# A conditioned transformer on one core: the layers' modulation vectors computed beside the merge and the first feed-forward

## The reference

```python
cond = jax.nn.silu(c)
for l in range(2):
    mod = (cond @ ada_w[l] + ada_b[l])[:, None, :]          # ada_w[l]: 1024 x 6144
    shift_m, scale_m, gate_m, shift_f, scale_f, gate_f = jnp.split(mod, 6, axis=-1)
    h = rms_norm(x, norm_mix_g[l]) * (1.0 + scale_m) + shift_m
    ...                                                     # projection of h, two attentions, gated sum: y
    x = x + gate_m * y
    h = rms_norm(x, norm_mlp_g[l]) * (1.0 + scale_f) + shift_f
    x = x + gate_f * (jnp.square(jax.nn.relu(h @ w_mlp_up[l])) @ w_mlp_down[l])
```

## Time and profile before

| | us |
|---|---|
| median of 3 runs | 3493.77 (3490.32 to 3534.7) |
| the profiled execution's own time | 3522.62 |
| its span in the profile | 3520.8 |
| TensorE busy, matmuls | 3085.6 (88% of the span) |
| VectorE busy | 1684.8 (48%) |
| ScalarE busy | 1032.7 (29%) |
| mean granted TensorE clock | 0.875 of full speed |
| read from memory | 243.70 MB, 70 GB/s over the span |

### The profile page before, as it was taken

The page is one execution under the profiler, slowest core; times in us unless marked ns, Lnnn a source line. Parts: engine busy times, 40 slices in busy tenths (PEclk is TensorE's granted clock), DMA queues, the critical chain, the costliest instruction groups (busy, mean ns, idle before and its releaser), DMA issues. The chain is left out here.

```text
span 3520.8 us, 36278 instructions
## 1 busy us (share of the span) xinstructions
PE 3085.6 (88%) x14073; PEld 2379.1 (68%) x14073; DVE 1684.8 (48%) x3186; ACT 1032.7 (29%) x2010; POOL 19.2 (1%) x58
## 2 busy tenths in 40 slices
PE   7969378886999579989999899997998999989999
PEld 5866267774887147657777688863765777768887
DVE  3223555555443656674233444455757623344444
ACT  2223211112332134543332322212445323232221
POOL 0000100000000000000000000000000000000000
PEclk9975577777999789989599999998999968989999
DMA  3210000001333532102023222245220211322221
GB/s 121 85 16 1 11 8 1 1 1 45 95 100 109 187 142 72 49 13 69 20 59 111 72 96 96 96 153 206 72 72 1 64 37 39 106 72 96 96 96 48
DMA packets 210677, 249.45 MB, mean 71 GB/s; under 512 B 11759, under 2 KB 124362, under 8 KB 210506
## 3 DMA queue, kind: packets, MB, share of 16 engines
q1 hardware_dynamic: 202016, 243.63, 21.0%
q10 hardware_dynamic: 8490, 3.50, 0.5%
HBM read 243.70 MB, written 2.10 MB: 70 GB/s over the span
## 5 line engine op out<-in xcount | busy, mean ns | idle before, releaser
L1804 DVE TENSOR_TENSOR weights_lo<-weight_ring,weights_hi 128x512 fp32r<-128x512 f32 (+1 forms) x240 | 156.8, 656 | 350.0 <-ACT weights_hi L1789 350.0
L1789 ACT ACTIVATE weights_hi<-weight_ring 128x512 fp32r<-128x512 f32 (+1 forms) x240 | 143.9, 602 | 423.3 <-PE bank L1824 398.1
L1824 PE MATMUL bank<-h_hi,weights_hi 128*128 128x512 f32 x512 | 208.4, 407 | 16.0 <-DVE h_lo L1804 9.1
L722 PE MATMUL bank<-arena 64*128 64x512 f32 (+4 forms) x544 | 207.1, 620 | 17.4 <-PEq L905 11.0
L2661 PE MATMUL bank<-h_hi,weights_hi 128*128 128x512 f32 x512 | 202.4, 395 | 19.4 <-DVE h_lo L342 19.4
L2161 PE MATMUL bank<-chunk_hi,h_hi 128*128 128x512 f32 x448 | 185.2, 413 | 30.4 <-DVE h_lo L342 26.0
L2592 ACT ACTIVATE weights_hi<-weight_ring 128x1024 fp32r<-128x1024 f32 x128 | 135.3, 1057 | 259.4 <-PE bank L2661 258.8
L1824 PE MATMUL bank<-h_lo,weights_hi 128*128 128x512 f32 x512 | 204.0, 398 | 0.0
L2661 PE MATMUL bank<-h_lo,weights_hi 128*128 128x512 f32 x512 | 203.9, 398 | 0.0
L1824 PE MATMUL bank<-h_hi,weights_lo 128*128 128x512 f32 x512 | 201.5, 394 | 0.0
L2661 PE MATMUL bank<-h_hi,weights_lo 128*128 128x512 f32 x512 | 201.2, 393 | 0.0
(11 more groups left out here) (447 smaller groups left out, 5932.2 us busy)
## 6 DMA issues: line engine op xcount, KB each, us to landing
weight_ring<-in_ada_w SPq DMA_DIRECT2D x24, 2048.0 KB, 8.9
weight_ring<-in_w_in SPq DMA_DIRECT2D x21, 2048.0 KB, 7.8
weight_ring<-in_w_in SPq DMA_DIRECT2D x65, 512.0 KB, 5.1
weight_ring<-in_w_mlp_up SPq DMA_DIRECT2D x16, 2048.0 KB, 8.4
weight_ring<-in_w_mlp_down SPq DMA_DIRECT2D x16, 2048.0 KB, 7.8
weight_ring<-in_w_out SPq DMA_DIRECT2D x6, 2048.0 KB, 7.9
weight_ring<-in_w_in SPq DMA_DIRECT2D x10, 1024.0 KB, 6.8
weight_ring<-in_w_branch_a SPq DMA_DIRECT2D x16, 512.0 KB, 6.3
```

Of the source, the lines that this page charges most:

```text
L722: ins = pe.matmul(self.bank[q % S_BANKS][:, lo:lo + m], lhsT, rhs, start=True, stop=True)
L1789: act.activation(hi, src, ACT.Copy).then_inc(*hi_done.one())
L1804: dve.tensor_tensor(lo, src, hi.bitcast(F32), ALU.subtract).then_inc(*lo_done.one())
L1824: ins = pe.matmul(out, ws[a_][:, n % PIECES, k - k0, :], tile["x"][b_][:, k, :], start=k + a_ + b_ == 0, stop=last[n] and k == k1 - 1 and ...
```

## The change

The two modulation stages go. A new class `Modulation` is a "guest" of another stage: that of layer 0 in the merge, that of layer 1 in the feed-forward of layer 0. Its weights come in 24 half chunks of 1 MB (4 slices x 512 columns) into two buffers of its own, by DMAs that ScalarE issues. VectorE does all eight slices of a chunk (96 multiplies a layer, one in each piece of the merge, two in each tile of the feed-forward up to the 48th). TensorE does twelve "turns" a layer: four matmuls with 128 x 128 columns of `acc` as the stationary operand and a column of ones as the one moving column, which sum over the partitions and turn the result in one go, into bank 7. The hosts rotate seven banks in place of eight. Bias and gains are computed at the end of the host stage. `cond` is computed in the stage `sg`, and the copy of `hT` to `xT` moves to the end of ScalarE's list in `layer_tables`.

```diff
     for l in range(2):
-        for c in range(12):
-            plan.append((("ada", l, c), [(columns(a["ada_w_2"][l], c * 512, 512), 0)]))
...
+class Modulation:
+    HALVES = 24
+    OPS = 4
+    def load(self, eng):
+        k, q = self.kernel, self.loads
+        c, half = q // 2, q % 2
+        if q >= 2:
+            eng.wait_ge(*k.ada_used.at(q - 1))
+        eng.dma_start(self.w[:, half], columns(self.source, 512 * c, 512, 4 * half, 4)).then_inc(*k.ada_landed[half].dma())
+        self.loads += 1
+    def multiply(self, dve):
+        k, n = self.kernel, self.ops
+        q, j = n // 4, n % 4
+        c, half = q // 2, q % 2
+        acc, by = self.acc[:, c % 2, :], k.cond[:, 4 * half + j:4 * half + j + 1]
+        if j == 0:
+            dve.wait_ge(*k.ada_landed[half].at(16 * (c + 1)))
+        if n % 8 == 0:
+            if c >= 2:
+                dve.wait_ge(*k.mod_turned.at(c - 1))
+            ins = dve.tensor_scalar(acc, self.w[:, half, j, :], by, None, ALU.mult)
+        else:
+            dve.wait_ge(*self.previous)
+            ins = dve.scalar_tensor_tensor(acc, self.w[:, half, j, :], by, acc, ALU.mult, ALU.add)
...
+    def turn(self, pe):
+        k, c = self.kernel, self.turns
+        pe.wait_ge(*k.ada_used.at(2 * c + 2))
+        for j in range(4):
+            ins = pe.matmul(k.bank[7][:, 4 * c + j:4 * c + j + 1], self.acc[:, c % 2, j * P:(j + 1) * P], k.ones[:, 0:1],
+                            start=True, stop=True)
+        ins.then_inc(*k.mod_turned.one())
+        self.turns += 1
+    def finish(self, dve):
+        dve.wait_ge(*k.mod_turned.at(self.HALVES // 2))
+        dve.tensor_tensor(mod, k.bank[7][:, 0:48], k.par[:, b:b + 48], ALU.add).then_inc(*k.mod_row.one())
...
@@ spatial gating, ScalarE, before the Ln @@
+                act.activation(self.cond, self.par[:, PAR["c_2"]:PAR["c_2"] + ND], ACT.Silu).then_inc(*self.act_order.one())
@@ split_products @@
+        NB = 7 if guest else 8
@@ ScalarE @@
+                for _ in range(2 if guest else 0):
+                    guest.load(act)
                 for n in range(len(pieces) + PIECES):
+                    if guest and n >= 6 and (n - 6) % 4 == 0 and guest.loads < guest.HALVES:
+                        guest.load(act)
@@ VectorE, between the wait for piece n - 4 and the split of piece n @@
+                        if guest and guest.ops < guest.HALVES * guest.OPS:
+                            guest.multiply(dve)
@@ TensorE, ahead of piece n @@
+                    if guest and n >= 10 and (n - 10) % 8 == 0:
+                        guest.turn(pe)
...
+                while guest and guest.turns < guest.HALVES // 2:
+                    guest.turn(pe)
@@ layer_tables, ScalarE @@
-                act.activation(self.cond, self.par[:, PAR["c_2"]:PAR["c_2"] + ND], ACT.Silu)\
-                   .then_inc(*self.act_ready.step("cond"))
+                for k in range(ND):
+                    act.activation(self.xT[:, k, :], self.hT[:, k, :], ACT.Copy).then_inc(*self.evac_act.one())
@@ layer @@
-        self.modulation(l)
@@ mlp, ScalarE, after the split of tile t + 1 @@
+                    if guest and t >= 3 and t % 2 and guest.loads < guest.HALVES:
+                        guest.load(act)
@@ mlp, VectorE, after the split of tile t + 1 @@
+                    for _ in range(2 if guest and guest.ops < guest.HALVES * guest.OPS else 0):
+                        guest.multiply(dve)
@@ mlp, TensorE, ahead of tile t @@
+                    if guest and t >= 6 and (t - 6) % 4 == 0 and guest.turns < guest.HALVES // 2:
+                        guest.turn(pe)
```

More of the change, by code:

```diff
@@ L342, in second_part, with __init__ @@
         return dve.scalar_tensor_tensor(lo, self.dst[:, k, :], self.shift(k), hi.bitcast(F32), ALU.add, ALU.subtract)
+class Modulation:
+    HALVES = 24
+    OPS = 4
+    def __init__(self, kernel, l):
+        self.kernel, self.l = kernel, l
+        self.w, self.acc = kernel.take(2, 4, 512), kernel.take(2, 512)
+        self.source = kernel.a["ada_w_2"][l]
+        self.loads = self.ops = self.turns = 0
+    def load(self, eng):
[19 more added lines that the diff above has]
+            ins = dve.scalar_tensor_tensor(acc, self.w[:, half, j, :], by, acc, ALU.mult, ALU.add)
+        done = k.ada_used if j == 3 else k.mod_row
+        ins.then_inc(*done.one())
+        self.previous = done.all()
+        self.ops += 1
+    def turn(self, pe):
[7 more added lines that the diff above has]
+    def finish(self, dve):
+        k, l = self.kernel, self.l
+        assert self.ops == 4 * self.HALVES
+        dve.wait_ge(*k.mod_turned.at(self.HALVES // 2))
+        b = PAR["ada_b_2"] + 48 * l
+        mod = k.mods[:, l, :]
+        dve.tensor_tensor(mod, k.bank[7][:, 0:48], k.par[:, b:b + 48], ALU.add).then_inc(*k.mod_row.one())
+        dve.wait_ge(*k.mod_row.all())
+        for j, (at, name) in enumerate(((8, "norm_mix_g_2"), (32, "norm_mlp_g_2"))):
+            g = k.par[:, PAR[name] + 8 * l:PAR[name] + 8 * l + 8]
+            dve.scalar_tensor_tensor(k.gains[:, l, j, :], mod[:, at:at + 8], 1.0, g, ALU.add, ALU.mult)\
+                .then_inc(*k.mod_row.one())
@@ L395, in __init__ @@
         self.scratch = sb("scratch", [P, 512])
+        self.cond, self.mods, self.gains = sb("cond", [P, ND])[:], sb("modulations", [P, 2, 48]), sb("mod_gains", [P, 2, 2, ND])
+        self.ada_landed = [Signal(nc, f"ada_landed_{j}") for j in range(2)]
+        self.ada_used = Signal(nc, "ada_used")
+        self.mod_row = Signal(nc, "mod_row_ready")
+        self.mod_turned = Signal(nc, "mod_turned")
         self.nc_pos = sb("positions", [P, NT], I32)
@@ L1717, in recurrences, with split_products @@
         self.end_stage("rwkv")
-    def split_products(self, name, tiles, inputs, norm=None):
+    def split_products(self, name, tiles, inputs, norm=None, guest=None):
         nc = self.nc
-        NB = 8
+        NB = 7 if guest else 8
         PK, PIECES = 4, 4
@@ L1868, in gated_sum @@
                 readers.append(b)
-        self.split_products(name, tiles, inputs, norm)
+        self.split_products(name, tiles, inputs, norm, guest)
         self.top -= 2 * T
@@ L1888, in merge @@
             inputs[2 * i + 1] = self.by_k(ysT, y)[2 * i:2 * i + 2]
-        self.gated_sum("merge", mixT, plan, inputs, self.norm)
+        keep = self.top
+        guest = Modulation(self, 0)
+        self.gated_sum("merge", mixT, plan, inputs, self.norm, guest)
+        self.top = keep
         self.add_products("out", lambda c: ("out", c), mixT, None)
@@ L2561, in layer @@
         self.top = keep
[L2562 removed]
+        self.rms(f"rms_mlp{l}", gain(1), mod(3))
         self.mlp(l, mod(5))
@@ L2663, in _ @@
                     ins.then_inc(*pe_done.one())
+                assert guest is None or guest.turns == guest.HALVES // 2
             @block.sync
```

90 lines of the change are left out of this document (13 added, 77 removed).

## The result

The changed kernel takes 3406.21 us (median of 4 runs, 3401.20 to 3410.06); beside it the kernel before took 3511.39 (4 runs: 3534.7, 3490.32, 3493.77, 3529.0). The ratio is 0.975 with a 95% interval of [0.971, 0.979]: faster. The forecast was 3375.0 in a range of 3350 to 3415, so direction and range held and the time was 31 us too low. The profiled execution of after took 3409.53 us, 113.1 less than the profiled one of before (3522.62); the prediction's sum for that pair was 118.8.

A forecast was written before the change was run, and what follows sets the result against it. TensorE bounds merge and feed-forward; the DMA-heavy modulation stages lie exposed. 3522.62 - 145.7 + 24.0 + 1.5 + 1.4 = 3403.8, 118.8 less; the same off the median 3493.77 gives 3375.0 us, range 3350 to 3415.

The forecast's parts named there:

- The stages removed: Layer 0's and layer 1's exposed modulation stages leave the critical path: 73.2 and 72.5 us, together 145.7 us saved.
- The turns: Twelve turns per layer added to TensorE in merge and feed-forward, 1.0 us each, 24.0 us in all, none hidden.
- the lower bound of 23.3: All 24 turns on TensorE at 0.97 us each, from one-column matmuls of 0.121 us with their load.
- The upper bound from the four-column matmuls at half clock: Turns on TensorE at the recurrence's 0.25 us a pair: 2.0 us a turn, 48.0 us in all.
- Rival (a): Turns in both hosts cost their upper bound, 2.0 us each: +24 us, 3399; chance 0.18.
- rival (b): In the turns, weight loads serialize with matmuls, 0.437 us a pair: +60 us, 3435, no measurable change; chance 0.04.
- VectorE, DMA and ScalarE at nothing: In both hosts, 192 multiplies, 48 loads of 1 MB and ScalarE's issues fit into idle time and cost nothing.
- Rival (c): Late-landing halves stall TensorE in both hosts: up to 229 us, 3604, loss beyond 13.5 us landings; chance 0.03.
- Starts and ends: Merge start 1.5 us for a landing wait and one multiply; bias and gains at both hosts' ends 1.4 us.
- The step that failed: Subtracting the profiled execution's saving of 118.8 us from the median of three timed runs, 3493.77, giving 3375.0.
- its upper side: Range above the forecast, to 3415: Rival (a) and as much again, with the merge's start at its bound.

## Why the prediction was right, and where it failed

**The stages removed**: right. 73.2 and 72.5 us forecast, 73.0 and 72.5 measured.

**The turns**: the mechanism is right, the size a little high. 1.0 us each was taken from the one-row matmuls and equal load times; 0.85 to 0.91 measured, so 24 turns are 20.4 to 21.8 us where 24.0 were summed, and the lower bound of 23.3 was too high. The upper bound from the four-column matmuls at half clock was far off, since these run at full clock: the timeline shows eight pairs in 0.81 us. Rival (a), 2.0 us each, and rival (b), load and matmul in series, 0.437 us a pair, are refuted by the same 0.81 us. The rule of the Trainium skill behind (b) ("TensorE: Matmul & The Clock Gate", "The mechanism" of Part 3, that a load overlaps only matmuls of another row group) does not describe these rows: with a load of 192 ns in each, eight pairs in series would take at least 1.5 us. (The same section of the Trainium skill also lets a load go ahead that targets the background weight buffer, which the prediction leaves out; whether that is at work here, no row shows.)

**VectorE, DMA and ScalarE at nothing**: right. The idle left in an up tile is 1.08 us where 0.97 was worked out, the loads land in 5.2 and 6.3 us, and with waits of up to 5.5 us for them the hosts grew by 0.8 and 0.0. Rival (c) has the right mechanism, and for the merge the right slack: put at 5.4 us, it let waits of 4.0 pass and not one of 5.54. One figure in support was wrong. A layer's modulation weights are 25.2 MB and not 12.6, so the merge was to be put at 93 + 115 = 208 GB/s instead of 151; 200 were measured, and the loads landed in time all the same.

**Starts and ends**: 1.5 us at the merge's start was for a landing that VectorE would wait for; it doesn't wait, and only the multiply's 0.40 us stands there. Beyond the turns, starts and ends hold 2.9 to 4.3 us of the hosts' 24.7, where 2.9 were summed; most of it in the feed-forward, which has 2.4 to 3.1 where 0.7 were given. Together the hosts cost 24.7 us where 26.9 were summed.

**The step that failed** is the last of the sum: "This execution is 28.9 above the median of the three timed runs, 3493.77; nothing removed depends much on the matmul clock, so I subtract the same from the median: 3375.0." The saving of 118.8 is right, its starting point isn't. The 28.9 us are no scatter about a middle. By their times two of the three timed runs had one dilated attention at the higher clock, which is worth 37 us; a profile shows it for the like execution of 3497.53, in which 12 of the 37 went again in longer recurrences (422.6 us against 410.5). Of all 42 executions of before, eleven lie under 3500. The profiled one was of the usual kind, and its own sum, 3403.8, is 5.7 us from after's profiled 3409.53 and 2.4 from the median 3406.21. So of the 31 us, 29 are this step; the rest is the 5.7 of stretches that the change leaves alone, less the 3.3 by which the profiled execution of after lies above its median.

The range took in the spread of the shown runs on its lower side alone. It held by 9 us, and that is luck: its upper side was room for dearer turns, which didn't come, and it was used up by the starting point. Nor does that side add up as told, since rival (a) is 24 us and "as much again" would be 48, while 3415 is 40 above the forecast.

**Luck in the measured ratio.** By their times none of the eight executions of after had such a stage, against about one in four of before. That the change made it rarer isn't shown: an execution with one guest had it in layer 0, and the runs with late loads reached down to 3364.

## What to carry to other kernels

Ask of each stage that is not bound by the engine you can't spare whether it can ride beside one that is; the price is then what it puts on the bound engine, and slack on the others can be worked out tile by tile; here it held as far as it was tried. When the timed runs of a kernel fall into two groups, find the stage that differs before you take a median as the starting point, and add a saving read from one profile to that profile's own time. Where TensorE is busy 99% of a stage at half clock behind a short idle, try a matmul that nobody reads in that idle: here one a layer cost nothing that could be read and gave 34 us, twice.

## What was not expected of the hardware

The granted clock of one and the same stage had two stable courses: 0.50 for 84.6 us with TensorE busy 83.6, or 0.99 for 55 us with it busy 51.4. The fall, where it came, came in the first microseconds behind idles of 0.94 and 0.91 us; but the stage that stayed up had idles of 0.94 and 0.92. Filling the second idle went with the higher level in all the executions that were profiled with a filling at the start (both layers of four kernels). A burst in mid-stage brought it back between 1651.33 and 1656.49. Whether the recurrences (granted clock 0.72 to 0.78 over their stretch, and the part of the kernel that varied most from run to run, 405 to 423 us) can be lifted so wasn't tried.

The Trainium skill ("TensorE: Matmul & The Clock Gate", Part 1) has the clock rise once TensorE has been busy. The row of 84.60 us disagrees: busy 99% by the profile, it didn't rise until matmuls of 128 rows and 512 columns were put in. What sets the stage's own matmuls apart from these, the 64 rows of the scores, the 64 to 384 moving columns or the operation, no run here separates.

A weight load of 128x128 and a matmul of one column, fp32, take 0.10 to 0.11 us a pair when eight follow each other, less than the 0.192 us that the profile gives the load alone (0.81 us for eight, where eight such loads in series are 1.54). So by the profile the loads overlap each other.
